# A chunked selective scan moved from behind the attention into the in-projection of a two-layer decoder trunk

## The reference, cut to what matters

```
z, xbc, dt = split(h @ w_in)                 # beside the columns of the two attention groups
xs, B, C  = split(silu(causal_dwconv(xbc)))  # 8 heads of 64; two groups of B and C, state 128
dt  = softplus(dt + bias);  a_h = cumsum(dt * -exp(a_log)) within each chunk of 128 tokens
decay  = exp(a_h[l] - a_h[s]) for s <= l
y_diag = (C B^T * decay) @ (xs*dt);  states = B^T @ (xs*dt * exp(a_h[end] - a_h))
h_next = h * exp(a_h[end]) + states          # eight chunks, one after the other
y = (y_diag + (C * exp(a_h)) @ h + xs*d_skip) * silu(z);  then an RMS norm per group
```

## Time and profile before

| | us |
|---|---|
| median of three runs | 2717.19 |
| the profiled execution | 2723.66 |
| its span | 2721.9 |
| PE busy in it | 2529.8 (93%) |
| DVE busy | 1450.6 (53%) |
| POOL busy | 1363.7 (50%) |
| ACT busy | 996.6 (37%) |

### The profile page before, as it was taken

One profiled execution on the slowest core, in us unless ns is written; L12 is line 12 of the kernel. 1 busy time (PEld: TensorE's weight loads), 2 busy tenths in 40 slices (PEclk: granted clock), 3 DMA queues, 4 the chain that ended last, 5 costly groups with the idle time before them and its releaser, 6 DMA issues. The chain is left out here.

```text
span 2721.9 us, 32828 instructions
## 1 busy us (share of the span) xinstructions
PE 2529.8 (93%) x12414; PEld 2060.8 (76%) x12414; DVE 1450.6 (53%) x1476; ACT 996.6 (37%) x1581; POOL 1363.7 (50%) x802
## 2 busy tenths in 40 slices
PE   4999988899999999999979998889989999999997
PEld 3888656787778888888868875577877888888886
DVE  7653266542855565655455326646266655555553
ACT  3233244431444344333222224435234444443232
POOL 3221793423487777444312139715229777754442
PEclk7998989789999999999979998878989999999998
DMA  6612341023132323364362224301212323226543
GB/s 234 209 47 51 99 124 48 32 74 97 39 95 71 93 78 86 133 219 144 115 210 52 59 61 124 100 32 48 70 62 80 85 78 93 70 86 216 168 149 109
DMA packets 227014, 274.87 MB, mean 101 GB/s; under 512 B 32568, under 2 KB 176797, under 8 KB 226077
## 3 DMA queue, kind: packets, MB, share of 16 engines
q1 hardware_dynamic: 226557, 271.88, 32.2%
q10 hardware_dynamic: 288, 0.79, 0.1%
HBM read 227.80 MB, written 44.04 MB: 100 GB/s over the span
## 5 line engine op out<-in xcount | busy, mean ns | idle before, releaser
L769 POOL TENSOR_TENSOR wLo<-raw,wHi 128x1024 fp32r<-128x1024 f32 x60 | 165.3, 2756 | 614.3 <-ACT wHi L771 613.1
L810 POOL TENSOR_TENSOR downLo<-raw,downHi 128x1024 fp32r<-128x1024 f32 x88 | 212.4, 2415 | 269.9 <-ACT downHi L817 269.9
L1952 DVE TENSOR_TENSOR gateLo<-gateRaw,gateHi 128x512 fp32r<-128x512 f32 x88 | 204.1, 2323 | 201.5 <-ACT gateHi L1564 201.5
L1307 POOL TENSOR_TENSOR prodLo<-comb,prodHi 128x512 fp32r<-128x512 f32 x160 | 221.4, 1389 | 144.9 <-ACT prodHi L803 144.9
L1195 PE MATMUL bank<-gateHi,downHi 128*128 128x512 f32 x704 | 274.2, 390 | 2.9 <-DVE gateLo L1952 2.9
L1195 PE MATMUL bank<-gateHi,downLo 128*128 128x512 f32 x704 | 273.9, 389 | 0.0
L1195 PE MATMUL bank<-gateLo,downHi 128*128 128x512 f32 x704 | 273.9, 389 | 0.0
L829 PE MATMUL bank<-hHi,wHi 128*128 128x512 f32 x768 | 245.0, 401 | 27.8 <-DVE hLo L1674 26.7
L1179 PE MATMUL bank<-tHi,prodHi 128*128 128x512 f32 x640 | 250.3, 391 | 7.9 <-DVE part L1948 4.0
L1179 PE MATMUL bank<-tHi,prodLo 128*128 128x512 f32 x640 | 249.7, 390 | 0.0
L1179 PE MATMUL bank<-tLo,prodHi 128*128 128x512 f32 x640 | 249.5, 390 | 0.0
(11 more groups left out here) (302 smaller groups left out, 5407.3 us busy)
## 6 DMA issues: line engine op xcount, KB each, us to landing
raw<-in_ffn_w_up_dram SPq DMA_DIRECT2D x88, 512.0 KB, 4.6
raw<-in_ffn_w_down_dram SPq DMA_DIRECT2D x88, 512.0 KB, 3.8
raw<-in_ada_w_dram SPq DMA_DIRECT2D x64, 512.0 KB, 3.9
gateOut<-ua SPq DMA_DIRECT2D x44, 512.0 KB, 3.3
gateRaw<-gateOut SPq DMA_DIRECT2D x88, 256.0 KB, 2.7
raw<-in_w_in_dram SPq DMA_DIRECT2D x36, 512.0 KB, 3.8
adaE<-in_ada_w_dram SPq DMA_DIRECT2D x32, 512.0 KB, 9.0
adaw<-in_ada_w_dram SPq DMA_DIRECT2D x16, 512.0 KB, 10.8
```

The source lines that it names most:

```text
L769: eng.tensor_tensor(wLo[slot][:], raw[slot][:], fview(wHi[slot][:]), ALU.subtract).then_inc(s["split_lo"], 1)
L810: eng.tensor_tensor(dwLo[slot][:], raw[kk % 2][:], fview(dwHi[slot][:]), ALU.subtract).then_inc(s["split_lo"], 1)
L1307: pool.tensor_tensor(sLoW[idx][:], product_source(js, idx), fview(sHiW[idx][:]), ALU.subtract).then_inc(s["us_lo"], 1)
L1952: dve.tensor_tensor(dgLo[kk % 4][:], gate_slot(kk)[:], fview(dgHi[kk % 4][:]), ALU.subtract).then_inc(s["g_lo"], 1)
```

## The change

It does nine things.

1. The tile with `dt` becomes tile 0 (64 columns are loaded where 8 were, so GpSimd's clearing of the gap goes), the second attention's tiles become 16 to 19, the convolution tiles 4 to 11 and z 12 to 15.
2. VectorE does `dt_work` first. The sixteen early products follow the taps of tiles 4 to 7, four each, and their weights are loaded into the space of `xT`, after its copy to `xtail` has landed.
3. The scan runs by chunks inside tiles 12 to 19. Chunk ch goes into tile 12+ch: `scan_state` after contraction step 2, `scan_scores` after step 4 (5 for chunk 0), `scan_back` after step 6, and at once `scan_turn` of the next chunk, which transposes x and B.
4. The running sum is no longer spread by TensorE. SyncE stores it to DRAM once (`cumOut`) and loads chunk by chunk a copy for all partitions (`load_spread`, 512 KB), from which ScalarE makes the decays; one buffer `cumSpread` serves all chunks, so the load of a chunk waits for the decays of the one before.
5. ScalarE makes the decays of the next chunk (`decays`) ahead of the weight copy `wHi` of the tile after next; exp and silu take turns in tiles 12 to 16.
6. GpSimd does `scan_decayed` (C), then `scan_ends` (the next chunk's x scaled with the decay to the end), then the weight remainder, then, from chunk 4 on, two gates each.
7. VectorE does per chunk: x times dt, the copy of B, the output of the chunk before, the state, and the two products with the scores.
8. The squares for the norm are made once by GpSimd (`scan_squares`), before `ada_products`. Their sums are 16 matmuls after the attention, ahead of the four `ada_sum`.
9. The blocks for the latent norms go after tiles 7 and 8; the two early `ada_sum` and the transposes of the step sizes after tile 9; the sum at the chunk's end after 10, and the turned values after the last tile.

The core of the diff (SP, PE, POOL, ACT, DVE in this order):

```diff
+                def load_spread(ch):
+                    if ch:
+                        sp.wait_ge(s["sd_seg"], 2 * ch)
+                        sp.wait_ge(s["sd_eb"], 2 * ch)
+                    sp.dma_start(spreadA[:], cum_out[:, ch, :, :].to_broadcast([P, 8, BLK])).then_inc(s["cum_loaded"], 16)
...
                     if n >= AHEAD:
                         load_pack(n, kind, m)
+                    if SCAN0 + 3 <= n < N_WIN:
+                        load_spread(n - SCAN0 - 2)
...
+                def scan_turn(ch):
...
+                    for j in range(4):
+                        pe.transpose(half(2, 0)[:, j * P:(j + 1) * P], xbc[:, j, chunk_cols(ch)], ident[:])
+                    for g in range(2):
+                        last = pe.transpose(half(2, 1)[:, g * P:(g + 1) * P], xbc[:, 4 + g, chunk_cols(ch)], ident[:])
...
+                def scan_state(ch):
...
+                    pe.wait_ge(s["sd_xe"], ch + 1)
...
+                    for g in range(2):
+                        last = mm(half(3, 0)[:, g * 256:(g + 1) * 256], bt[:, g, :], xe[:, 4 * g:4 * g + 4, :], start=True, stop=True)
...
+                def scan_back(ch):
+                    pe.wait_ge(s["sd_M"], 2 * ch + 2)
+                    pe.wait_ge(s["sd_cs"], 2 * ch + 2)
...
+                def scan_after(m):
...
+                    return {2: [(scan_state, ch)], 4: [(scan_scores, ch)],
+                            6: [(scan_back, ch)] + ([(scan_turn, ch + 1)] if ch + 1 < NB else [])}
...
-                sd_front(0)
-                sd_front(1)
-                for v in range(2 * NB):
-                    sd_back(v)
-                    if v + 2 < 2 * NB:
-                        sd_front(v + 2)
...
+                def scan_part(ch):
+                    scan_decayed(ch)
+                    if ch + 1 < NB:
+                        scan_ends(ch + 1)
+                    if SCAN0 + 2 + ch < N_WIN:
+                        split_pre(pool, SCAN0 + 2 + ch)
+                    for done in ((0, 1), (2, 3), (4, 5), (6, 7))[ch - 4] if ch >= 4 else ():
+                        scan_gate(done)
...
+                def decays(ch):
+                    act.wait_ge(s["cum_loaded"], 16 * (ch + 1))
+                    if ch:
+                        act.wait_ge(s["sd_yd"], ch)
+                    for g in range(2):
+                        for q in range(4):
+                            h = 4 * g + q
+                            last = A(Mt[g][:, q, :], spreadA[:, h, :], ACT.Relu, bias=adt[:, ch, h:h + 1], scale=-1.0)
+                        last.then_inc(s["sd_seg"], 1)
+                        A(Cs[g][:], spreadA[:, 4 * g:4 * g + 4, :], ACT.Exp).then_inc(s["sd_eb"], 1)
+                        act.wait_ge(s["sd_seg"], 2 * ch + g + 1)
+                        A(Mt[g][:], Mt[g][:], ACT.Exp, scale=-1.0).then_inc(s["sd_dec"], 1)
...
+                for ch in range(NB):
+                    if ch:
+                        scan_turned(ch)
+                        chunk_out(ch - 1)
+                    if ch < NB - 1:
+                        next_state(ch)
+                    for g in range(2):
+                        mix(ch, g)
+                chunk_out(NB - 1)
```

More of the change, by code:

```diff
@@ L191, in build @@
     yLo = place("ssdLo", [P, 4, T], F32R, E[8])
-    adaE = [place(f"adaE{k}", [P, D], F32, E[8 + k]) for k in range(KT)]
+    adaE = [place(f"adaE{k}", [P, D], F32, at["x"] + 4 * K * k) for k in range(KT)]
     R = [at["h"] + 4 * K * i for i in range(16)]
@@ L831, in dense_step, with dense @@
                     return last
-                def dense(pair, w_hi, w_lo, r_hi, r_lo, kts):
+                def dense(pair, w_hi, w_lo, r_hi, r_lo, kts, after={}):
                     for k in range(kts):
                         last = dense_step(pair, k, w_hi, w_lo, r_hi, r_lo, k == 0, k == kts - 1)
+                        if k < kts - 1:
+                            for part_, ch in after.get(k, ()):
+                                part_(ch)
                     return last
@@ new lines, in scan_back @@
+                def scan_back(ch):
+                    pe.wait_ge(s["sd_M"], 2 * ch + 2)
+                    pe.wait_ge(s["sd_cs"], 2 * ch + 2)
+                    pe.wait_ge(s["sd_h"], 1 + 2 * ch)
+                    if ch:
+                        pe.wait_ge(s["sd_yd_read"], ch)
+                    for h in range(SSD_HEADS):
+                        g, q = divmod(h, 4)
+                        o = half(3, 1)[64 * (h % 2):64 * (h % 2) + 64, (h // 2) * P:(h // 2 + 1) * P]
+                        mm(o, xd[:, h, :], Mt[g][:, q, :], start=True, stop=False)
+                        last = mm(o, hst[ch % 2][:, h, :], Cs[g][:, q, :], start=False, stop=True)
+                    last.then_inc(s["sd_yd"], 1)
@@ L1031, in _ @@
                 pe.wait_ge(s["ml_x"], NB)
+                pe.wait_ge(s["sd_sq"], 6)
+                for g in range(2):
+                    for b in range(NB):
+                        last = mm(half(2, 1)[:, 256 + NB * g + b:257 + NB * g + b], xbc[:, 4 + 2 * g, b * P:(b + 1) * P], ones, start=True, stop=True)
+                last.then_inc(s["sd_ss"], 1)
                 for j in range(2, 6):
                     ada_sum(j)
-                pe.wait_ge(s["dt_ready"], 1)
-                pe.wait_ge(s["mod_rest"], 3)
@@ L1288, in _ @@
[L1288 to L1289 removed]
+                    split_pre(pool, n)
                 def combos(js):
@@ L1508, in _ @@
[L1508 to L1510 removed]
+                for m in range(2):
+                    split_pre(act, N_OUT0 + m)
+                root(half(2, 1)[:, 256:256 + 2 * NB], rst[:], SSD_INNER // 2, "sd_ss", "sd_rstd")
                 for j in range(4):
@@ L1705, in dt_work, with early_product @@
                     last.then_inc(s["dt_ready"], 1)
-                for r in range(2 * KT):
+                def early_product(r):
                     j, k = divmod(r, KT)
@@ new lines, in chunk_out @@
+                def chunk_out(ch):
+                    c0 = slice(ch * BLK, (ch + 1) * BLK)
+                    dve.wait_ge(s["sd_yd"], ch + 1)
+                    for j in range(4):
+                        last = dve.scalar_tensor_tensor(out=xbc[:, j, c0], in0=xbc[:, j, c0], scalar=dcol[:, j:j + 1],
+                                                        in1=half(3, 1)[:, j * P:(j + 1) * P], op0=ALU.mult, op1=ALU.add)
+                    last.then_inc(s["sd_yd_read"], 1)
+                for ch in range(NB):
+                    if ch:
+                        scan_turned(ch)
+                        chunk_out(ch - 1)
+                    if ch < NB - 1:
+                        next_state(ch)
+                    for g in range(2):
+                        mix(ch, g)
```

483 lines of the change are left out of this document (224 added, 259 removed).

## The result

The changed kernel takes 2630.95 us (median of 4 runs, 2628.49 to 2632.98), the kernel before on the same chip 2716.49 (2715.13 to 2720.36). The ratio is 0.9682, with a 95% interval from 0.9666 to 0.9698: 85.5 us less, where 62.1 were forecast.

The account below looks back on a forecast made before the run. TensorE, busy 93% of the span, was taken as the bound. Moved work, waits, clock falls and smaller terms cost 54.9 us per layer against 84.4 and 87.5 removed: 62.1 gained, median 2655 us, 8-in-10 range 2622 to 2696.

Parts of the forecast that it names:

- likeliest case: The forecast itself: 62.1 us gained over both layers, median 2655 us, own range 2638 to 2672, chance 0.50.
- first rival: In the eight tiles TensorE's waits stay hidden: 4 us per layer, no fall of the clock, 2626 us; chance 0.17.
- The stage removed and the work that moves with it: Scan stage's 84.4 and 87.5 us go; its products cost 33.3 us per layer in the tiles, step-size transposes and chunk-end sum 1.4.
- Waits: TensorE's waits inside the eight tiles, from three chains on other engines: 11.8 us per layer, ends 4 and 25.
- two `Mt` products (mean 1.49): VectorE's chain after the scores takes 3.7 us with signals against TensorE's 2.7, a wait of 1.0 us per chunk.
- The clock: Two falls of TensorE's clock per layer, at chunk 0 and chunks 5 and 6, 3.4 us each: 6.8, bounds 0 and 27.
- The rule weighed: A VectorE operation with two SBUF inputs and a GpSimd operation take a shared port pair in turns, each for the whole instruction.
- second rival: VectorE and GpSimd take turns beside both `Mt` products, each waiting about 0.8 us more: 26 us more, 2681; chance 0.15.
- Hidden with 0.6 us to spare: The running sum's load per chunk, queued behind the weight tile's, lands at T + 15.0 and is wanted at T + 15.6.
- slow ring: Decays, weight copy, remainder, load and decays again make each chunk 2.5 us longer: 40 us more, 2695; chance 0.13.
- Latent norms: The 3.32 us wait before their spread goes and the spread falls from 5.43 to about 3.7 us: -5.0 per layer.
- Column sums: After the attention sixteen new one-column sums of the squares, 32 rows, cost 5.8 us per layer, 7.0 at most.

Follow-up runs that it names:

- small `Cdec`: Changed kernel with GpSimd making only 8 of 128 columns per head of the `Cdec` products, so its output is not the reference's; measured once, 2627.55 us.
- scores late: Changed kernel with the score products directly ahead of the outputs from chunk 1 on; 2656.35 us, ratio 0.9774 to the kernel before.
- undone order: Changed kernel with GpSimd scaling the next chunk behind the weight remainder instead of ahead of it; 2692.0 us, ratio 0.9905 to the kernel before.
- load ahead: Changed kernel with the running sum's load ahead of the weight tile's in SyncE's order; 2626.11 us, ratio 0.9647 to the kernel before.
- scores early: Changed kernel with the score products one contraction step earlier from chunk 1 on, after step 3 instead of 4; 2627.99 us, ratio 0.9676.

## Why the prediction was right, and what was off

It said 2655, faster, and a range from 2622 to 2696; 2631 lies in it, below the likeliest case's own range of 2638 to 2672 and near the first rival's 2626. The direction and the mechanism were right, two terms of the sum were too large: the waits lie between that rival's 4 and the forecast's 11.8, and the clock is as that rival had it.

- **The stage removed and the work that moves with it.** Right within 5%, from durations of single products: 34.7 forecast, 33.0 and 33.5 measured, with the 1.3 us ahead of the scan taken off in layer one. What is measured is the remainder of the account, not a sum of instructions.
- **Waits.** 11.8 forecast, 7.6 and 7.1 measured. The step that failed is "two `Mt` products (mean 1.49)", which gave 1.0 us per chunk. All the products behind that mean were slow ones. In chunks 1 to 3 the products now take 1.80 and 0.69, 2.5 instead of 3.0, and the wait is 0.4; in chunk 7 both take 0.69, and the 1.0 forecast there is nothing. The kernel with the small `Cdec` showed which of them is due to GpSimd. Chunks 0, 5 and 6 were named as the long ones and are: 1.3, 3.0 and 1.0 against 3.1, 2.3 and 1.4. Chunk 4 was not named; its 1.1 comes from the load.
- **The clock.** 6.8 forecast, nothing measured in either of the two profiled executions of the changed kernel. The step read a fall in the old scan stage and carried it to "chunk 0 and chunks 5 and 6", two per layer at 3.4 us. The price was too high: falls cost 1.6 us each with the scores late and 2.2 with the undone order. The count is in part luck. Waits of 2.97 and 2.59 us left the clock at 1.00 here; in kernels close to it a wait at the same place brought a fall: 2.32 us with the load ahead, in both layers; 2.92 with the small `Cdec` (0.69 from 309.5 to 315 us); 3.83 with the scores early (0.73 from 311.7 to 318). Waits of 4.2 us brought one ten times of ten. That dense products fill eleven of sixteen us is a likely reason why most short waits cost nothing, but no run varies it, and the length of the wait alone does not decide.
- **The rule weighed.** The trace of after bears out what the Trainium skill, page "SBUF — State Buffer", section "Who interferes with whom", says, closer than the row of before did: the product beside `Cdec` ended 0.5 us after it. The second rival failed all the same: in chunks 1 to 3 only one of the two `Mt` products stands beside GpSimd, and in chunks 4 to 6, where both do, they take 1.2 to 1.74 us each, about the mean that the sum had used already.
- **The load.** "Hidden with 0.6 us to spare" was right in chunks 1 to 3 and short in chunks 4 and 5, where the weight tile comes in two parts and the load waits behind two issues. The slow ring, a rival with a chance of 0.13, was real and near, though at a load of 4.8 us and not the 8 to 10 that it supposed: taking 0.4 us out of each chunk was enough to bring it up.
- **Latent norms.** -5.0 forecast, -5.2 measured, and VectorE was in time (its reciprocal at 166.77, the spread at 176.48).
- **Column sums.** The squares' 5.8 was 4.9. But the 64 modulation rows behind them grew from 11.6 to 13.65 us, since they now stand wholly in the slow stretch; the prediction had this growth nowhere. The two together cost 7.0 and 6.6. That this is near the 7.0 which the prediction gave as the squares' upper end is luck.
- **GpSimd behind the in-projection.** Cost nothing, as forecast: its last product of the modulation ended at 498.9, 15 us before the sums.

## What to carry to other kernels

When work is put into the gaps of a dense stage, price each wait from the instruction's two durations, alone (0.69 us here) and beside the engine that it shares SBUF with (1.80), not from a mean over a stage in which it never ran alone. Look for the next chain behind the one that sets the wait: here shortening one by 0.4 us gave nothing, and together with two more edits, one of them an earlier load, it removed all waits but those of one chunk. Waits of 2 to 3 us between dense products cost a fall of the clock sometimes, of some 1.6 us, those of 4.2 us each time, and an order on a third engine decided which kind it was. Read a clock in both layers and in more than one execution before a rule is made of it.

## What was not expected of the hardware

- One-column fp32 rows cost 0.113 us each at 2.4 GHz (32 in 3.63 us at 190.96) and 0.21 at 1.2. Dense products between groups of them brought the clock back in one of four cases; in another it was 0.50 through 25 us in which TensorE was never idle. In tile 9, with dense products on both sides, the clock was 1.00 through 32 such rows and fell right behind them, 0.58 from 194.5 to 198 us, again without any wait:

```profile
196.20 1.05 PE L850 MATMUL bank<-hLo,wHi 128*128 128x512 f32 x2
```

- A VectorE product of 0.69 us took up to 2.57 beside GpSimd's remainder (scores early, from 287.84; it ended 0.55 us after the remainder), and two `Cdec` products took 3.45 instead of 2.53 in the same kernel (at 256.69): both engines lose.
